# The last token tile turned ahead of its LayerNorm, with its router logits corrected afterwards; a second route batch of two tiles; 512 columns a product in output tiles 2 to 4

## The reference

```python
x <- LN1(alpha*x + Mixer(x));  x <- LN2(alpha*x + HierMoE(x))

# end of the mixer
merged = sigmoid(g_hg) * br_hg + sigmoid(g_att) * br_att
out = merged @ w_out
# layer_norm: (x - mu) * rsqrt(var + 1e-5) * g + b

# hier_moe: 4 groups x 4 experts, width 256
g_logits = xt @ w_rg + b_rg                      # 4 columns
g_w = softmax(g_logits)[argmax]                  # top 1 of the groups
e_logits = (xt @ w_re + b_re) of that group      # 16 columns in all
top_p, top_i = top_k(softmax(e_logits), 2)       # top 2 in the group, renormalised
y = sum of w_down(silu(xt w_gate) * (xt w_up)) * g_w * top_p
```

## Time and profile before

| | us |
|---|---|
| median of 3 runs | 827.02 |
| lowest and highest of them | 824.53, 830.73 |
| the profiled execution's own time | 824.47 |
| its span, first to last instruction | 822.5 |
| PE busy | 740.1 (90%) |
| DVE busy | 555.3 (68%) |
| ACT busy | 391.7 (48%) |
| mean granted TensorE clock | 0.952 |

### The profile page before, as it was taken

The page is one execution under the profiler, slowest core; times in us unless marked ns, Lnnn a source line. Parts: engine busy times, 40 slices in busy tenths (PEclk is TensorE's granted clock), DMA queues, the critical chain, the costliest instruction groups (busy, mean ns, idle before and its releaser), DMA issues.

```text
span 822.5 us, 13533 instructions
## 1 busy us (share of the span) xinstructions
PE 740.1 (90%) x5359; PEld 648.1 (79%) x5359; DVE 555.3 (68%) x1020; ACT 391.7 (48%) x651; POOL 43.7 (5%) x39
## 2 busy tenths in 40 slices
PE   6999999999999999888899999998459988899784
PEld 5989999999998999666678999998447766676531
DVE  4244966888644877998753565755648888888537
ACT  4348752558327332344555432111237877778502
POOL 0000000000000000000000000000010111010064
PEclk8999999999999999999999999999569999999977
DMA  7333122221333241332101963812427999999263
GB/s 235 103 112 101 52 70 86 66 68 26 122 108 116 66 148 53 116 129 69 67 29 42 351 232 107 299 45 83 160 77 255 378 389 386 385 387 386 68 230 115
DMA packets 92799, 129.86 MB, mean 158 GB/s; under 512 B 8576, under 2 KB 75136, under 8 KB 92736
## 3 DMA queue, kind: packets, MB, share of 16 engines
q1 hardware_dynamic: 87072, 112.21, 40.2%
q0 software_dynamic: 3360, 12.06, 4.2%
q10 hardware_dynamic: 2304, 4.72, 1.5%
HBM read 109.02 MB, written 19.81 MB: 157 GB/s over the span
## 4 chain that ended last, share of the span: by engine, by line
PE 67%; DVE 14%; issue 7%; ACT 6%; DMA 5%; SPq 1%; POOL 0%; ACTq 0%; DVEq 0%; POOLq 0%
PE pp L813 25%; PE pw L1134 12%; PE pp L1011 5%; PE pp L1157 5%; PE pp L793 3%; PE pw L871 2%; ACT w_hi L1226 2%; DVE w_lo L1672 2%; PE pp L1120 2%; DVE Lm L1861 1%; PE pw L980 1%; PE pw L1198 1%; DMA xtok<-in_x_sample_dram 1%; PE pp L769 1%; PE pw L1033 1%
## 5 line engine op out<-in xcount | busy, mean ns | idle before, releaser
L813 PE MATMUL pp<-x_hi,w_hi 128*128 128x288 f32 (+1 forms) x608 | 187.8, 309 | 2.6 <-DVE w_lo L1672 1.2
L813 PE MATMUL pp<-x_lo,w_hi 128*128 128x288 f32 (+1 forms) x608 | 179.6, 295 | 0.0
L813 PE MATMUL pp<-x_hi,w_lo 128*128 128x288 f32 (+1 forms) x608 | 179.4, 295 | 0.0
L813 PEld LDWEIGHTS pp<-x_hi,w_hi 128*128 128x128 f32 (+1 forms) x608 | 114.9, 189 | 10.6 <-issue 7.6
L813 PEld LDWEIGHTS pp<-x_lo,w_hi 128*128 128x128 f32 (+1 forms) x608 | 113.9, 187 | 0.2
L813 PEld LDWEIGHTS pp<-x_hi,w_lo 128*128 128x128 f32 (+1 forms) x608 | 113.7, 187 | 0.0
L1672 DVE TENSOR_TENSOR w_lo<-w_raw,w_hi 128x2048 fp32r<-128x2048 f32 (+1 forms) x30 | 67.1, 2236 | 43.7 <-ACT w_hi L1226 43.5
L2103 DVE TENSOR_TENSOR glo<-wgu,ghi 128x1024 fp32r<-128x1024 f32 x64 | 76.6, 1219 | 19.0 <-ACT ghi L1502 18.8
L1502 ACT ACTIVATE ghi<-wgu 128x1024 fp32r<-128x1024 f32 x64 | 65.7, 1052 | 22.4 <-DMA wgu<-in_w_up_dram 22.4
L1134 PE MATMUL pw<-ghi,xTh 128*112 128x512 f32 x128 | 53.2, 416 | 14.7 <-issue 12.3
L1226 ACT ACTIVATE w_hi<-w_raw 128x2048 fp32r<-128x2048 f32 (+1 forms) x30 | 56.0, 1865 | 5.7 <-ACT gring L1262 4.1
(11 more groups left out here) (327 smaller groups left out, 1662.2 us busy)
## 6 DMA issues: line engine op xcount, KB each, us to landing
w_raw<-in_w_in_dram SPq DMA_DIRECT2D x23, 1024.0 KB, 5.5
wgu<-in_w_gate_dram SPq DMA_DIRECT2D x16, 1024.0 KB, 11.3
wgu<-in_w_up_dram SPq DMA_DIRECT2D x16, 1024.0 KB, 14.5
wd<-in_w_down_dram SPq DMA_DIRECT2D x16, 1024.0 KB, 9.0
ys_d<-ysb SPq DMA_DIRECT2D x16, 448.0 KB, 11.2
gates_d<-gring ACTq DMA_DIRECT2D x16, 288.0 KB, 2.1
w_raw<-in_w_out_dram SPq DMA_DIRECT2D x4, 1024.0 KB, 6.5
gates_early<-gates_d SPq DMA_DIRECT2D x4, 576.0 KB, 4.0
```

Source lines behind the costliest of these rows:

```text
L813: mm = pe.matmul(pp[0:wide, b, 0:HT], lw, rx, start=(k == 0 and y == 0), stop=(k == last and y == 2))
```

## The change

Five things change.

1. Output tiles 0 and 1 keep their groups of 256 columns. In tiles 2 to 4, `out_group(i, j, 2)` covers two column blocks with one product of 512 columns.
2. The turns and routers of tiles 0 to 3 are placed by hand between the groups. The first batch has tiles 0 to 2, the second tiles 3 and 4. Both batches' ranks get a PSUM bank of their own.
3. Tile 4 is turned as it is after the residual, before LN1. Its router uses `w * g` (`wgb`), and the logits become `rstd * (x @ (w g)) + nmr * sum(w g) + sum(w b) + bias`, with `nmr = -mean * rstd`. The two column sums are eight products with ones (`router_sums`). `g` and `b` are loaded once more in a column layout (`gb`), 4 bytes a piece.
4. ACT copies the turned tile 4 ahead of all pieces of expert 0's high part. On DVE the one-hots of batch 0 come after route(1), three of the four `gate_up_low` pieces come after `stok`, and `weights()` is split in two.
5. `Mt` and `hot` are declared float32r, so that the products of `slot_tokens` take one pass.

```diff
-BATCHES = [(0, 2), (2, 5)]
+BATCHES = [(0, 3), (3, 5)]
...
+        gb = ra("gb", [P, 2, KD])
-        Mt = ra("Mt", [P, 2, NT, NX])
+        Mt = ra("Mt", [P, 2, NT, NX], F32R)
-        hot = ra("hot", [P, 2, NT, P])
+        hot = ra("hot", [P, 2, NT, P], F32R)
+        wgb = wa("wgb", [P, KD, 40])
+        csb = wa("csb", [P, 40])
...
+            for n, row in enumerate((ln1_g, ln1_b)):
+                sp.dma_start(gb[:, n, :], row.rearrange("a (k p) -> p (a k)", p=P), allow_slow_non_contiguous=True).then_inc(s_rc, 16)
...
-            def out_group(i, j):
+            def out_group(i, j, wide):
...
+                        w = rw(OUT0 + j)[:, k, :] if wide == 1 else out_pair(rw, j)[:, :, k, :]
+                        mm = pe.matmul(pp[0:r, 2 * b + j // 2, GW * (j % 2):GW * (j % 2 + wide)], lx[:, k, i * P:i * P + r],
+                                       w, start=(k == 0 and y == 0), stop=(k == KD - 1 and y == 2))
+            def router_sums():
+                pe.wait_ge(s_wgb, 2)
+                for k in range(KD):
+                    mm = pe.matmul(pw[:, 3, 448:488], ones[:], wgb[:, k, :], start=(k == 0), stop=(k == KD - 1))
+                mm.then_inc(s_sums, 1)
             def turn_x1(i):
-                pe.wait_ge(s_x1, i + 1)
+                if i < NT - 1:
+                    pe.wait_ge(s_x1, i + 1)
+                else:
+                    pe.wait_ge(s_res, i + 1)
...
+            for t, j in ((0, 0), (1, 0), (0, 1), (1, 1)):
+                out_group(t, j, 1)
+            for t, j in ((0, 2), (0, 3), (1, 2), (1, 3)):
+                out_group(t, j, 1)
+            out_group(2, 0, 2)
+            turn_x1(0)
+            out_group(2, 2, 2)
+            router(0)
+            turn_x1(1)
+            router_sums()
+            out_group(3, 0, 2)
+            router(1)
+            turn_x1(2)
+            out_group(3, 2, 2)
+            router(2)
+            out_group(4, 0, 2)
+            turn_x1(3)
+            out_group(4, 2, 2)
+            router(3)
+            ranks(0)
+            turn_x1(4)
+            router(4)
+            ranks(1)
             slot_tokens(0)
-            turn_x1(NT - 1)
-            router(NT - 1)
-            ranks(1)
             slot_tokens(1)
...
-            for n in range(PIECES - 1):
+            x1_copy(NT - 1)
+            for n in range(PIECES):
                 gate_up_high(0, n)
-            x1_copy(NT - 1)
-            gate_up_high(0, PIECES - 1)
...
+                if end == NT:
+                    link(ins)
+                    ins = dve.scalar_tensor_tensor(lg[:, NT - 1, :], pw[:, 2, 80:100], rstd[:, NT - 1:NT], lgc[:], ALU.mult, ALU.add)
...
+            def router_weights():
+                for n in range(2):
+                    dve.tensor_tensor(wgb[:, :, 20 * n:20 * n + 20], wr[:], gb[:, n, :].unsqueeze(2).broadcast_to([P, KD, 20]), ALU.mult).then_inc(s_wgb, 1)
+            def last_sums():
+                dve.wait_ge(s_sums, 1)
+                link(dve.tensor_copy(csb[:, 0:20], pw[:, 3, 448:468]))
+                link(dve.tensor_tensor(csb[:, 20:40], pw[:, 3, 468:488], br_[:], ALU.add))
+            def last_shift():
+                i = NT - 1
+                inverse_root(i, P, s_sd)
+                link(dve.scalar_tensor_tensor(nmr[:, i:i + 1], mv[:, i, 0:1], -1.0, rstd[:, i:i + 1], ALU.mult, ALU.mult))
+                link(dve.scalar_tensor_tensor(lgc[:], csb[:, 0:20], nmr[:, i:i + 1], csb[:, 20:40], ALU.mult, ALU.add))
+            def last_normal():
+                i = NT - 1
+                x = xr[0:64, i, :]
+                dve.wait_ge(s_tx, 2 * NT)
+                link(dve.scalar_tensor_tensor(x, x, mv[0:64, i, 0:1], lnr[0:64, 0, :], ALU.subtract, ALU.mult))
+                dve.scalar_tensor_tensor(x, x, rstd[0:64, i:i + 1], lnr[0:64, 1, :], ALU.mult, ALU.add).then_inc(s_x1, 1)
             for i in range(NT):
                 residual(i)
                 moments(i, xr[:, i, :], P, s_var)
-                normalize(i)
+                if i == 0:
+                    router_weights()
+                if i < NT - 1:
+                    normalize(i)
                 if i == BATCHES[0][1]:
+                    last_sums()
                     route(0)
-                if i == BATCHES[0][1] + 1:
-                    one_hot_ranks(0)
-            for n in range(PIECES):
-                gate_up_low(0, n)
+            last_shift()
+            last_normal()
             route(1)
+            one_hot_ranks(0)
             one_hot_ranks(1)
+            gate_up_low(0, 0)
             dve.wait_ge(s_id, len(BATCHES))
...
-            weights()
+            gate_up_low(0, 1)
+            weights_first()
+            for n in range(2, PIECES):
+                gate_up_low(0, n)
+            weights_last()
```

More of the change, by code:

```diff
@@ L400, in encoder_layer @@
         w_lo = lambda g: wl[:, g % 2] if g < OUT0 + 2 else wol[:, g - OUT0 - 2]
+        assert OUT0 % 2 == 0
+        out_pair = lambda part, j: ((wh if part is w_hi else wl) if j == 0 else (woh if part is w_hi else wol))
         pwf = [pw[:, 2 * b:2 * b + 2].rearrange("p a b -> p (a b)") for b in range(2)]
@@ L1002, in out_group @@
                 if i == 0:
-                    weights_ready(OUT0 + j)
-                if (i, j) in TURNS:
-                    turn_x1(TURNS[i, j])
+                    for n in range(j, j + wide):
+                        weights_ready(OUT0 + n)
                 for k in range(KD):
@@ L1032, in router @@
                 for k in range(KD):
-                    mm = pe.matmul(pw[:, 2, 20 * i:20 * i + 20], x1T[:, i % 2, k, :], wr[:, k, :], start=(k == 0), stop=(k == KD - 1))
+                    mm = pe.matmul(pw[:, 2, 20 * i:20 * i + 20], x1T[:, i % 2, k, :], wr[:, k, :] if i < NT - 1 else wgb[:, k, 0:20],
+                                   start=(k == 0), stop=(k == KD - 1))
                 mm.then_inc(s_logit, 1)
@@ L1050, in ranks @@
                 pe.wait_ge(s_M, b + 1)
-                if b:
-                    pe.wait_ge(s_hot, b)
                 at, upto = NX * first, NX * end
+                bank = pw[:, 3 - b, 128 * b:]
                 flat = lambda t: t.rearrange("p i e -> p (i e)")
                 if first == 0:
-                    pe.matmul(pw[:, 3, at:NX], lower[:], M[:, 0, :], start=True, stop=True)
+                    pe.matmul(bank[:, at:NX], lower[:], M[:, 0, :], start=True, stop=True)
                     first, at = 1, NX
-                pe.matmul(pw[:, 3, at:upto], lower[:], flat(M[:, first:end, :]), start=True, stop=False)
-                mm = pe.matmul(pw[:, 3, at:upto], ones[:], flat(before[:, first:end, :]), start=False, stop=True)
+                pe.matmul(bank[:, at:upto], lower[:], flat(M[:, first:end, :]), start=True, stop=False)
+                mm = pe.matmul(bank[:, at:upto], ones[:], flat(before[:, first:end, :]), start=False, stop=True)
                 if end == NT:
-                    mm = pe.matmul(pw[:, 3, upto:upto + NX], ones[:], before[:, NT, :], start=True, stop=True)
+                    mm = pe.matmul(bank[:, upto:upto + NX], ones[:], before[:, NT, :], start=True, stop=True)
                 mm.then_inc(s_rk, 1)
@@ L2019, in route @@
                 col = lambda c: cols[:, c, tl]
+                whole = min(end, NT - 1)
                 dve.wait_ge(s_logit, end)
-                dve.tensor_tensor(lg[:, tl], pw[:, 2, 20 * first:20 * end].rearrange("p (i c) -> p i c", c=20),
-                                  br_[:].unsqueeze(1).broadcast_to([P, n, 20]), ALU.add).then_inc(s_lgd, 1)
+                ins = dve.tensor_tensor(lg[:, first:whole], pw[:, 2, 20 * first:20 * whole].rearrange("p (i c) -> p i c", c=20),
+                                        br_[:].unsqueeze(1).broadcast_to([P, whole - first, 20]), ALU.add)
+                if end == NT:
+                    link(ins)
+                    ins = dve.scalar_tensor_tensor(lg[:, NT - 1, :], pw[:, 2, 80:100], rstd[:, NT - 1:NT], lgc[:], ALU.mult, ALU.add)
+                ins.then_inc(s_lgd, 1)
                 dve.wait_ge(s_lgd, b + 1)
@@ L2056, in one_hot_ranks @@
                 tl = slice(first, end)
-                ranks_ = pw[:, 3, NX * first:NX * end].rearrange("p (i e) -> p i e", e=NX)
+                bank = pw[:, 3 - b, 128 * b:]
+                ranks_ = bank[:, NX * first:NX * end].rearrange("p (i e) -> p i e", e=NX)
                 dve.wait_ge(s_rk, b + 1)
@@ L2084, in weights, with weights_last @@
                 dve.tensor_copy(dest[:], destf[:]).then_inc(s_dest, 1)
+            def weights_last():
+                wide = lambda t: t.unsqueeze(2).broadcast_to([P, NT, 4])
+                col = lambda c: cols[:, c, :]
                 dve.wait_ge(s_ge, 2)
```

29 lines of the change are left out of this document (11 added, 18 removed).

## The result

The changed kernel takes 817.56 us (median of 4 runs, 814.73 to 819.77) against 825.99 (4 runs, 824.53 to 830.73): ratio 0.9881, 95% interval 0.9855 to 0.9908. Measured again beside the later experiments, the ratio was 0.9908 (0.9875 to 0.994). The profiled execution took 816.84 us, its span is 814.7.

What follows compares the result with a forecast made beforehand. Bound taken: TensorE up to 570.97 us, then a 35.8 us serial tail to the first expert product, whose shift moves the whole expert stage. Terms +0.1 - 5.4 - 1.1 + 0.2 = -6.2 us; forecast 820.0 us, range 814.5 to 826.5.

Steps and rivals of the forecast that it cites:

- Part 1: Output stage from 517.27 us to E: wide products -1.0, router sums +1.74, ranks(0) -0.65, clock 0; sum +0.1 us.
- rival A: Clock holds after the router sums (-1.45) and for router(4) (-1.0): saving 8.7, 815.8 or 818.3 us; chance 0.26 with somewhat beyond.
- Part 2: From E to tile 4's router logits: 8.0 us instead of 13.4, -5.4 us.
- E: As a time: end of tile 4's last output product. As a rival: 4-byte loads come late, 823.0 us, chance 0.04.
- Part 3: From the logits through route(1) to slot tokens ready: 12.1 us instead of 13.2, -1.1 us.
- Part 4: Slot tokens to expert 0's first product: VectorE's list becomes as late as the gather, 9.4 us for 9.2, +0.2 us.
- Cover of VectorE ahead of E: VectorE is free 12.8 us after tile 3's end, TensorE reaches E after 13.6: 0.8 us to spare.
- Part 5: SP queue: two loads of 4-byte elements ahead of the constants take 2.3 us, within 3.1 us of room; cost 0.
- Rival D: Expert stage: loads set their own time, so the first expert product moves but the end does not; 827 us, chance 0.06.
- B: Clock falls in each of three further output groups (4.35 us), E's tail 1.1: saving 0.8, 826.2 us; chance 0.11 with mixtures.
- C: Lower clock holds from the router sums to E: 13.0 us slower, 840.0 us; chance 0.05 with other slower ends.

Runs made afterwards that it cites:

- narrow: The changed kernel with output tiles 2 to 4 back in groups of 256 columns; 818.38 us, ratio 0.991 to the kernel before.
- adjacent: The changed kernel with turn(1) moved behind the router sums, so router(0) and the sums stand side by side; 817.53 us, ratio 0.9888.
- after_again: The changed kernel unaltered, measured and profiled a second time; 819.7 us, ratio 0.9908 to the kernel before.
- fill: The changed kernel with 29 unused TensorE products added between tile 4's last output product and expert 0; 814.73 us, ratio 0.9853.
- late4: The changed kernel with tile 4 turned only after its LN1 and its router on the plain weights; 824.94 us, ratio 0.9983.
- early: The changed kernel with route batches of tiles 0 to 1 and 2 to 4, batch 0's ranks and one-hots earlier; 818.99 us, ratio 0.9896.
- delay: The changed kernel with five useless statistics operations, 3.7 us, on VectorE ahead of the slot tokens; 822.56 us, ratio 0.9945.
- wide_only: The kernel before with only the 512-column products in tiles 2 to 4, turn(1) behind tile 2; 826.11 us, ratio 0.9983.
- fill2: The changed kernel with more unused TensorE products behind router(4), and the weights' last part behind the tokens' low part on VectorE; 815.41 us, ratio 0.9866.
- lows_first: The changed kernel with all four low parts of expert 0's gate and up weights ahead of route(1); 822.05 us, ratio 0.9942.

## Why the prediction was right, and what it mis-sized

The forecast was 820.0 in 814.5 to 826.5; 817.56 lies in it. The sum said 6.2 us, the trace shows 7.9 up to the first expert product (8.4 in the second profile of the changed kernel), and the medians 8.4. Two things beside the sum entered the time: the clock in the first two gate-and-up groups, worth -2.1 us in one profile of the changed kernel and +0.5 in the other, and the median of before, 827.02 in three runs and 825.99 with the fourth. How near the time came to 820.0 is in part luck; the parts are what the prediction is to be judged by.

**Part 1** was the mis-sized one. Wide products: -1.0 predicted, -0.8 by narrow, and nothing in tile 4, as said. Router sums +1.71 for +1.74, ranks(0) -0.67 for -0.65. The clock was the error: I kept the fall of the earlier trace rows at full price, and it did not come, -1.45. Together -1.2. That is the first half of rival A. The reason that I gave against it, that router(0), turn(1) and the sums are longer than the run that made the clock fall, did not hold; with the turn behind the sums it did fall, in the one profile of adjacent.

By the Trainium skill's gap (TensorE: Matmul & The Clock Gate, Back-to-back issue gap), columns over the clock plus about 2.5 ns, the wide products would be worth an estimated 0.36 us. The Trainium skill gives it for a product by itself; for a stream of weight loads and products it has about 131 ns at 512 columns, and the rows here have 232 ns. The trace agrees with neither: the four groups of tiles 2 and 3 are 0.12 to 0.26 us shorter than in narrow for 24 merged pairs each, 5 to 11 ns a pair, 0.8 us in all.

**Part 2** held, -5.7 for -5.4. Turn at 2.4 behind E, copy at 3.3, router(4) at 4.4 are as worked out (573.36, 574.30, 575.38). Router(4) met the fall half-way, 3.21 us for 3.62, so the logits came at 7.6, not 8.0; in after_again it met none, 1.96 us, and they came at 7.2. The premise that the products behind E are alike in both kernels was not right: before, TensorE stood idle for 4.08 us ahead of tile 4's turn at 577.62 and the clock was 0.67 in 573 to 575, now it turned tile 4 up to 574.28 and the clock was 1.00 there. LN1's last pass ends at 7.3; after_again and fill show that a full clock for router(4) gives no more than this. Late4 confirms the part from the other side, 6.4 us.

**Part 3**: -1.2 for -1.1. The one-hots of batches 0 and 1 took 2.2 and 2.0 us, as worked out. Early shows where the gain is not: with the batches of before the part is 12.1 us, so the second batch of two is worth 0.1 to 0.2 of the 1.2. The products of `slot_tokens` are 10 instructions in all for 20 before, and in early the last ones take 1.46 us on the chain where before took 2.76; that this is the rest is argued from the rows, since no run tests the float32r operands by themselves. **Part 4**: +0.25 for +0.2, though not by VectorE's list: the copy behind the gather came last, with a gather of 4.57 us for 4.31.

**Cover of VectorE ahead of E.** Residual(4) waited 1.01 us for TensorE, for a predicted cover of 0.8.

**Part 5** held. SP's queue after:

```profile
508.47 0.37 SPq L584 DMA_DIRECT2D w_raw<-in_w_out_dram  x1
508.89 0.57 SPq L663 DMA_DIRECT2D gb<-in_ln_g_dram  x1
509.52 1.20 SPq L663 DMA_DIRECT2D gb<-in_ln_b_dram  x1
510.76 2.72 SPq L669 DMA_DIRECT2D wr<-in_w_rg_dram  x1
...
517.68 0.43 SPq L669 DMA_DIRECT2D tidf<-in_c_tidf_dram  x1
```

The two loads hold the queue for 0.57 and 1.20 us, and the constants' last issue comes 9.2 us behind the last `w_out` load instead of 7.7, 1.5 later, for 2.3 predicted. Residual(0) still waited for TensorE, 3.37 us, so this costs the chain nothing. The Trainium skill (DMA: Bandwidth & Descriptors, Rules for kernel authors) has one descriptor per element for such a non-contiguous last dimension. The trace agrees: the packets of the hardware queues rise from 87,072 to 89,152, 1,040 for each of the two loads of 1,024 elements.

**What follows.** Rival D is refuted by delay and by the two profiles after: 215.8 and 216.0 us from the first expert product to the end before, 214.7 and 216.9 after. The prediction took this distance as fixed; it is not, as the two gate-and-up groups show. B, C and E did not occur.

**Open.** What makes the clock fall in the output stage is not settled. It fell in both profiles of before and in adjacent; it did not in wide_only twice, nor in narrow, late4, delay, early, fill, fill2, lows_first and the two of after, where a turn parts router(0) and the sums. Neither "routers in a row" nor "narrow products around them" alone fits all of these, and adjacent was profiled once. Nor is it settled what sets the clock in expert 0's and expert 1's first groups, which together take 11.6 to 16.0 us in the 14 profiles and move the end with them.

## What to carry to other kernels

Where a serial chain of small operations separates two dense stages, a linear operation at its head can be taken ahead of the normalisation and corrected afterwards with two column sums; here that shortened the chain by 5.7 us for 1.7 us of extra products. Whether that reaches the end is read from what releases the following stage: here its loads are issued by the stage's own progress and moved with it, as delay showed with 3.2 us. Once the wait is gone, what used to be hidden in it (here four low parts, 4 us) is on the path and has to be moved behind the next wait.

## What the runs showed of the hardware that was not expected

Giving TensorE 29 useless products in the 29 us between two dense stages gave 5.0 us of 819.7 by the medians and 3.3 by the profiled executions, in runs on one chip, though no step up to the next stage came earlier: the first two gate-and-up groups ran at the upper clock, 5.8 us each, where the changed kernel's two profiles have 7.24 and 5.80, and 8.22 and 7.34. A further 1.5 us earlier start (fill2) was lost again where expert 1's group met the lower clock, so that such a gain is not a sure one.

The fall of the clock behind 3.5 us of small products, with TensorE at work throughout, costs 1.45 to 1.5 us and came back in the same place in both profiles of the kernel before (72 products in 10.18 and 10.19 us).
